# Branch and output projections of a diffusion block as three rounded products in place of plain fp32

## What is computed

```python
def branch_merge(y_a, y_b, y_c, gates, w_pa, w_pb, w_pc, w_out):
    g_a, g_b, g_c = jnp.split(gates, N_BRANCHES, axis=-1)
    m = (jax.nn.sigmoid(g_a) * (y_a @ w_pa) + jax.nn.sigmoid(g_b) * (y_b @ w_pb)
         + jax.nn.sigmoid(g_c) * (y_c @ w_pc))
    return m @ w_out
...
for layer in range(DEPTH):
    hx = modulate(rms_norm(x, norm1_g[layer]), sh1, sc1)
    mx, mc = token_mixers(hx @ w_in[layer], hc @ w_in[layer], ...)   # three branches, then branch_merge
    x = x + g1 * mx
    hx = modulate(rms_norm(x, norm2_g[layer]), sh2, sc2)
    # layer 0: dense SwiGLU of 2816; layer 1: top 2 of 8 expert SwiGLUs of 3584
    x = x + g2 * f
return rms_norm(x, final_g)
```

## Time and profile before

| | |
|---|---|
| Median of 3 runs | 2270.48 us (2268.6 to 2272.04) |
| Profiled execution, time | 2268.39 us |
| Profiled execution, span from first to last instruction | 2266.5 us |
| Mean granted clock of TensorE | 0.968 |
| PE busy | 2140.1 us, 94% |
| POOL busy | 1272.5 us, 56% |
| DVE busy | 1147.7 us, 51% |
| ACT busy | 1051.7 us, 46% |
| Read from memory | 500.24 MB |

### The profile page before, as it was taken

One profiled execution on the slowest core, in us unless ns is written; L12 is line 12 of the kernel. 1 busy time (PEld: TensorE's weight loads), 2 busy tenths in 40 slices (PEclk: granted clock), 3 DMA queues, 4 the chain that ended last, 5 costly groups with the idle time before them and its releaser, 6 DMA issues.

```text
span 2266.5 us, 27521 instructions
## 1 busy us (share of the span) xinstructions
PE 2140.1 (94%) x10750; PEld 1589.7 (70%) x10751; DVE 1147.7 (51%) x1353; ACT 1051.7 (46%) x1139; POOL 1272.5 (56%) x466
## 2 busy tenths in 40 slices
PE   5988899998999998887998999999999999999997
PEld 3874577647788787864997777776767777776775
DVE  2146311231010103345324887878778787878776
ACT  4223322014212123323324766766666666766665
POOL 2300233114545443400421989988988989988996
PEclk8999999998999999898997999999999999999999
DMA  7325521222222222225445999989999999989993
GB/s 296 111 94 223 207 93 75 75 74 103 102 80 106 77 91 93 92 104 205 162 162 204 371 337 353 358 334 352 346 341 345 347 340 351 357 333 352 346 346 142
DMA packets 69640, 503.16 MB, mean 222 GB/s; under 512 B 7744, under 2 KB 7872, under 8 KB 9088
## 3 DMA queue, kind: packets, MB, share of 16 engines
q1 hardware_dynamic: 68976, 497.92, 58.8%
q0 software_dynamic: 528, 3.41, 0.4%
HBM read 500.24 MB, written 1.05 MB: 221 GB/s over the span
## 4 chain that ended last, share of the span: by engine, by line
PE 49%; POOL 32%; issue 12%; DVE 3%; DMA 2%; ACT 1%; SPq 0%; POOLq 0%; DVEq 0%; ACTq 0%
POOL moe_lo L482 31%; PE bank L756 12%; PE bank L758 11%; PE bank L757 11%; PE bank L771 7%; PE bank L784 2%; PE turned L955 2%; PE pv_bank L974 1%; DMA start_slab<-in_w_mod 1%; PE bank L934 1%; DVE s_mx L1859 1%; DMA slab<-in_w_in 1%; POOL w_lo L446 1%; ACT H_NEW L1359 0%; PE bank L939 0%
## 5 line engine op out<-in xcount | busy, mean ns | idle before, releaser
L482 POOL TENSOR_TENSOR moe_lo<-moe_slab,moe_hi 128x512 fp32r<-128x512 f32 x336 | 916.0, 2750 | 163.1 <-ACT moe_hi L1543 161.8
L482 DVE TENSOR_TENSOR moe_lo<-moe_slab,moe_hi 128x1536 fp32r<-128x1536 f32 x336 | 688.3, 2053 | 175.0 <-ACT moe_hi L1543 172.6
L446 POOL TENSOR_TENSOR w_lo<-slab,w_hi 128x2048 fp32r<-128x2048 f32 (+3 forms) x72 | 293.1, 4072 | 741.8 <-ACT w_hi L1316 741.7
L1543 ACT ACTIVATE moe_hi<-moe_slab 128x2048 fp32r<-128x2048 f32 x336 | 629.5, 1906 | 0.1
L756 PE MATMUL bank<-moe_hi,HE_HI 128*96 128x512 f32 x896 | 360.3, 402 | 1.3 <-POOL moe_lo L482 1.2
L758 PE MATMUL bank<-moe_hi,HE_LO 128*96 128x512 f32 x896 | 353.1, 394 | 0.0
L757 PE MATMUL bank<-moe_lo,HE_HI 128*96 128x512 f32 x896 | 351.7, 392 | 0.0
L756 PE MATMUL bank<-H_HI,w_hi 128*128 128x512 f32 (+1 forms) x880 | 325.6, 370 | 17.9 <-POOL H_LO L660 12.7
L757 PE MATMUL bank<-H_LO,w_hi 128*128 128x512 f32 (+1 forms) x880 | 321.9, 366 | 0.0
L758 PE MATMUL bank<-H_HI,w_lo 128*128 128x512 f32 (+1 forms) x880 | 321.8, 366 | 0.0
L1316 ACT ACTIVATE w_hi<-slab 128x2048 fp32r<-128x2048 f32 (+1 forms) x72 | 135.6, 1883 | 166.6 <-PE bank L758 147.8
(11 more groups left out here) (199 smaller groups left out, 2481.9 us busy)
## 6 DMA issues: line engine op xcount, KB each, us to landing
moe_slab<-in_moe_up SPq DMA_DIRECT2D x224, 1024.0 KB, 4.8
moe_slab<-in_moe_w SPq DMA_DIRECT2D x112, 1024.0 KB, 4.8
slab<-in_w_mod SPq DMA_DIRECT2D x40, 1024.0 KB, 4.8
slab<-in_w_in SPq DMA_DIRECT2D x38, 1024.0 KB, 4.8
slab<-in_ffn_w SPq DMA_DIRECT2D x30, 1024.0 KB, 4.8
start_slab<-in_w_mod SPq DMA_DIRECT2D x8, 1024.0 KB, 18.0
slab<-in_w_proj SPq DMA_DIRECT2D x8, 1024.0 KB, 6.9
slab<-in_w_out SPq DMA_DIRECT2D x8, 1024.0 KB, 4.9
```

What stands on the lines that cost most here:

```text
L446: engine.tensor_tensor(lo, raw, hi.bitcast(F32), ALU.subtract).then_inc(done, 1)
L482: engine.tensor_tensor(moe_lo[n][:, blocks, :], moe_slab[k % MOE_RING][:, blocks, :], moe_hi[n][:, blocks, :].bitcast(F32), ALU.subtract). ...
L1543: af(moe_hi[k % MOE_SPLIT][:], moe_slab[k % MOE_RING][:], ACT.Copy).then_inc(moe_hi_ready, 1)
```

## The change

The branch and output slabs become split slabs: every slab except those for the modulation now passes through `w_hi` and `w_lo`, eight more in each layer, and in layer 1 DVE makes half of each low part. `Y` is cut into `Y_HI` (ACT, four instructions of two chunks) and `Y_LO` (DVE, four, in place of `Y`). `M` shrinks to two chunks that are used again for each j; ACT rounds them into `M_HI` and DVE subtracts into `M_LO`. PE makes three products where it made one. The first output slab is worked through for both halves up to chunk 5 before the last two chunks are waited for.

`M_LO` takes the place of `BIAS` and `POOL` in SBUF. So both are loaded for layer 1 again (the matrix thus twice in all), now from SP's queue after the last output slab of layer 0. Three slabs of the expert stream are loaded ahead of the last output slab's end, as the ring places come free, where it was four. The rounding of slab w3(0,0) moves behind the root in the norm; that of stream slab 1 too, in layer 1, with DVE's part of it between the norm's TMPs.

```diff
 def is_split(slab):
-    return slab[0] in ("in", "w1", "w3", "w2")
+    return slab[0] != "mod"
...
+SHARED += [(kind, 1, j) for kind in ("proj", "out") for j in range(4)]
...
+        Y_LO = at("Y_LO", 56, [P, DC, T], F32R)
+        Y_HI = at("Y_HI", 168, [P, DC, T], F32R)
-        M = at("M", 72, [P, DC, T])
+        M = at("M", 164, [P, 2, T])
+        M_HI = at("M_HI", 72, [P, DC, T], F32R)
+        M_LO = at("M_LO", 148, [P, DC, T], F32R)
...
             for n in range(1, len(order)):
+                if order[n] == ("w3", 0, 1):
+                    wait_full(sp, ("out", 0, 3, 1))
+                    sp.dma_start(POOL[:]..., a["pool_mat"]).then_inc(pool_in[1], 16)
+                    sp.dma_start(BIAS[:]..., a["rel_bias"][1]).then_inc(bias_in[1], 16)
                 load_slab(n, order[n])
...
-            wait_full(sp, ("gate", 1, 3, 2, 1))
-            for k in range(MOE_RING - RING):
+            for k in range(RING):
+                wait_parts(sp, ("out", 1, 4 - RING + k))
                 stream_load(k)
...
-                    (w,) = slab(("proj", layer, j))
+                    w = slab(("proj", layer, j))
                     if j == 0:
-                        pe.wait_ge(y_ready[layer], len(attention_pairs(layer)))
-                        ...
+                        pe.wait_ge(y_lo_ready[layer], DC // 2)
...
-                            filled(chain(out[:, 0:nq], [(w[:, k, P * m:P * m + P], Y[:, k, 0:nq]) ...
+                            filled(split_chain(out[:, 0:nq], [
+                                ([t[:, k, P * m:P * m + P] for t in w], [t[:, k, 0:nq] for t in (Y_HI, Y_LO)])
+                                for k in BRANCH_CHUNKS[b]]), key)
...
-                wait_taken(pe, ("proj", layer, 3, 2, 1))
+                w = slab(("out", layer, 0))
+                outs = [fill(("out", layer, 0, m)) for m in range(2)]
+                pe.wait_ge(m_lo_ready[layer], DC - 2)
+                for m in range(2):
+                    for k in range(DC - 2):
+                        out_products(outs[m], w, m, k)
+                for k in range(DC - 2, DC):
+                    pe.wait_ge(m_lo_ready[layer], k + 1)
+                    ...
...
-                if key == (1, 1):
+                if key in ((0, 2), (1, 1)):
                     high_part()
+                if key == (1, 2):
+                    stream_high(1)
...
+                for k in range(0, DC, 2):
+                    af(Y_HI[:, k:k + 2, 0:nq], Y[:, k:k + 2, 0:nq], ACT.Copy).then_inc(y_hi_ready[layer], 1)
...
-                        if 3 * j + b < 10:
-                            high_part()
+                        high_part()
+                    if j < 3:
+                        high_part()
+                        m_rounded(j)
+                    else:
+                        m_rounded(j)
+                        high_part()
...
-                squares((layer, 2), lo, hi, range(0, 4), out_added)
+                squares((layer, 2), lo, hi, range(0, 2), out_added)
+                high_part()
+                squares((layer, 2), lo, hi, range(2, 4), out_added)
+                high_part()
...
+                    if key == (1, 2) and c == 2:
+                        stream_low_part(dve, v, 1, slice(0, LO_DVE), moe_lo_dve)
...
+                    if norm_key == (1, 2) and c in (1, 3):
+                        low_half(("out", 1, 2 + c // 2))
...
+                for k in range(0, DC, 2):
+                    dve.wait_ge(y_hi_ready[layer], k // 2 + 1)
+                    v.tensor_tensor(Y_LO[:, k:k + 2, 0:nq], Y[:, k:k + 2, 0:nq], Y_HI[...], ALU.subtract)
...
+                    if j == 3:
+                        m_low()
+                    if layer == 1:
+                        low_half(slabs[4 * j + 5])
+                    if j < 3:
+                        m_low()
```

More of the change, by code:

```diff
@@ L704, in _ @@
             h_low_parts((1, 1))
-            for _ in range(2, 19):
+            for _ in range(2, 27):
                 next_low_part()
@@ L1481, in merge, with m_rounded @@
                 nq = S * len(streams_of(layer))
+                act.wait_ge(y_ready[layer], len(attention_pairs(layer)))
+                for p in range(2):
+                    wait_taken(act, ("poolw", layer, p))
+                for k in range(0, DC, 2):
+                    af(Y_HI[:, k:k + 2, 0:nq], Y[:, k:k + 2, 0:nq], ACT.Copy).then_inc(y_hi_ready[layer], 1)
+                def m_rounded(j):
+                    for m in range(2):
+                        wait_taken(act, ("proj", layer, j, 2, m))
+                        af(M_HI[:, 2 * j + m, 0:nq], M[:, m, 0:nq], ACT.Copy).then_inc(m_hi_ready[layer], 1)
                 for j in range(4):
@@ L1626, in out_added @@
                     wait_taken(act, ("out", layer, c // 2, c % 2))
-                squares((layer, 2), lo, hi, range(0, 4), out_added)
+                squares((layer, 2), lo, hi, range(0, 2), out_added)
+                high_part()
+                squares((layer, 2), lo, hi, range(2, 4), out_added)
+                high_part()
+                squares((layer, 2), lo, hi, range(4, 6), out_added)
                 if layer == 0:
@@ L1633, in _ @@
                     stream_high(0)
-                squares((layer, 2), lo, hi, range(4, 6), out_added)
-                if layer == 0:
-                    high_part()
-                else:
-                    stream_high(1)
                 squares((layer, 2), lo, hi, range(6, 8), out_added)
@@ L1906, in merge @@
                 nq = S * len(streams_of(layer))
-                gates = [W_IN_GATE + 4 * b + j for j in range(4) for b in range(3)]
+                slabs = []
+                for j in range(4):
+                    slabs += [("in", 1, W_IN_GATE + 4 * b + j) for b in range(3)] + [("proj", 1, j)]
+                slabs += [("out", 1, j) for j in range(2)]
                 if layer == 1:
-                    low_half(gates[0])
-                    low_half(gates[1])
+                    low_half(slabs[0])
+                    low_half(slabs[1])
+                for k in range(0, DC, 2):
+                    dve.wait_ge(y_hi_ready[layer], k // 2 + 1)
+                    v.tensor_tensor(Y_LO[:, k:k + 2, 0:nq], Y[:, k:k + 2, 0:nq], Y_HI[:, k:k + 2, 0:nq].bitcast(F32),
+                                    ALU.subtract).then_inc(y_lo_ready[layer], 1)
                 for j in range(4):
                     if layer == 1:
-                        for slab in gates[3 * j + 2:3 * j + 5]:
-                            low_half(slab)
+                        for key in slabs[4 * j + 2:4 * j + 5]:
+                            low_half(key)
                     for b in range(3):
```

76 lines of the change are left out of this document (45 added, 31 removed).

## The result

The changed kernel takes 2233.26 us, median of 4 runs (2228.61 to 2241.9), beside 2269.54 us for the kernel before (4 runs, 2268.34 to 2272.04): a ratio of 0.985 [0.981, 0.988]. The direction was right, the time was not. The same two kernels were run more often beside the experiments: in all 37 runs of before have a median of 2266.2 (2261.4 to 2272.0) and 9 of after one of 2235.3 (2228.2 to 2241.9). The difference of these is 30.9 us.

The account below looks back on a forecast made before the run. PE, busy 94% of the span, was taken as the bound. -34.9 + 1.5 + 0.6 + 0.2 + 2.6 + 0.4 = -29.6 us from 2268.39 gave 2238.8, and 2.1 for the median 2241; range 2235 to 2249.

Parts of the forecast that it names:

- PE's part, layer 0: Layer 0's four branch and four output slabs at the gate slabs' price: 23.1 us less, plus M's wait covered.
- (d): New products escape the 11 ns each gate matmul loses, 4 us in all: 2237; chance 0.03.
- (e): The new form brings PE nothing, as 48 loads of weights stand where 32 did: 2270; chance 0.03.
- Layer 1: Eight slabs 9.2 us less, M's wait 1.0 less; stalls for low parts add 0.6, 0.2 and 2.6.
- rival (c): Layer 1 becomes bound by conversions, each rounding 0.7 us later over 17 slabs: 12 us, 2253; chance 0.10.
- The norm after layer 0: Slab w3(0,0)'s low part stands ahead of H_LO in POOL's queue, so H_LO's first chunk and PE are later: +1.5 us.
- from there ... nothing gives the delay back: After H_LO's late first chunk PE is busy without a gap, at first at 1.2 GHz, so the 1.5 us stay.
- The norm before the experts: DVE's 1.75 us part of stream slab 1 between the TMPs delays H's chunk 2: about +0.4 us, bounds 0 and 1.75.
- rival (b): The expert stream misses its fourth slab loaded early: +3.1 us, 2244; chance 0.10.
- Rival (f): DVE and POOL exclude each other when both read two SBUF tiles, 4.6 us in each new layer 0 slab: +37, 2278; 0.04.
- M's subtractions end before the next low part starts: Layer 0's output phase: DVE's subtractions into M_LO finish before POOL's next low part, an argument against DVE and POOL excluding each other.
- The median of the runs stands 2.1 higher, so I predict 2241: Last step: the profiled execution less 29.6 us gives 2238.8; the runs' median stands 2.1 above it, hence 2241.

Follow-up runs that it names:

- DVE's larger share: The changed kernel with DVE making three quarters, not half, of each gate, branch and output slab's low part in layer 1: 2232.96 us, ratio 0.986 to the kernel before.
- The two orders on POOL: The changed kernel (2235.3 us), and the same with POOL making H_LO's first chunks ahead of slab w3(0,0)'s low part in layer 0's second norm: 2235.03 us.
- the two halves: Kernel before with only branch projections as three rounded products, 2252.64 us; with only output projections so, plus the second loads for layer 1, 2245.0 us.

## Why the prediction was right in its steps and wrong in its time

**PE's part, layer 0.** Forecast 24.7 (23.1 and 1.6 of M's wait), measured 24.7 in all three traces of the change; from the first branch product to the last output product 184.7 us, forecast 185. The plain slabs' prices in the chain and the gates' spacing were enough. Rivals (d) and (e) fall with the 226 ns.

**Layer 1.** Forecast -9.2 - 1.0 + 0.6 + 0.2 + 2.6 = -6.8, measured -5.8; first branch product to last output product 103.4, forecast 102. The waits for w_lo in the output phase are 1.9 and 0.6, forecast 2.0 and 0.6. The missing 1 us is no single term. By the starts of the products in the first pair, products and M's wait give 9.9 (forecast 10.2), the second and fourth output slab come 2.2 and 0.8 late (2.6 together in the forecast), and the shorter delays are 2.9 beside 2.0 before (forecast +0.8). PE's busy time fell by 7.6 and not by 9.2, since most of the short delays stand in the rows as longer matmuls (as 0.39 beside 0.28 in the earlier trace rows). With DVE's larger share the stage is 9.6 shorter than before, nearly the full 10.2. So rival (c) names the right resource; it had 12 us more than the sum, and 1 was measured.

**The norm after layer 0.** Forecast +1.5, and at equal clock (13.7 us at 1.2 GHz in both) the FFN's first product starts 12.7 us after the last output product did, 11.3 to 11.5 before: +1.3. (Counted from that product's end, as the forecast of 12.4 was, it is 12.3.) But the first SiLU is only 0.75 later. The step "from there ... nothing gives the delay back" failed by half. The stretch at 1.2 GHz lasts from 3.2 to 16.8 us after the last output product's start before the change and from 2.9 to 16.6 after it, so a first product at 11.5 finds 5.4 us of it and one at 12.7 finds 3.9; at 0.44 each that is an estimated 0.7 given back. In the two other traces of the change the slow stretch is 10.2 and the first SiLU no later than before (23.2). The two orders on POOL come out level because slab w3(0,0)'s own low part has a due time too.

**The norm before the experts.** Forecast +0.4, measured +0.9 at equal clock (34.25 against 33.4), inside its bounds of 0 and 1.75. The loads: neither FFN nor stream became longer, so rival (b) and the second loads of `BIAS` and `POOL` cost nothing that shows.

**Rival (f), exclusion of DVE and POOL.** It is there, off PE's path. Timelines of DVE and POOL in the changed kernel's layer 0, two subtractions of M and the low part of a slab beside them:

```profile
397.07 5.29 DVE L1990 TENSOR_TENSOR M_LO<-M,M_HI 128x512 fp32r<-128x512 f32 x2 [1.04 <-ACT M_HI L1520]
...
396.60 4.61 POOL L456 TENSOR_TENSOR w_lo<-slab,w_hi 128x2048 fp32r<-128x2048 f32 x1 [5.86 <-ACT w_hi L1343]
```

The row merges two subtractions: the first takes 4.69 and ends 0.55 after POOL does, the second 0.68. The prediction's "M's subtractions end before the next low part starts" is thus wrong for three of the eight, the first of each pair but the last; nobody waits for these, as the output slabs come 40 us later and more. The last pair, which is wanted soonest, ran alone (0.69 each).

**The sum.** Stage by stage: -24.7 - 5.8 + 0.75 + 0.9 = -28.9, beside -29.6 forecast, -30.9 between the medians of 37 and 9 runs, and -36.3 between the medians of the first four runs of each. The forecast of the edit was right; what made the first pair 36 was in no term of it.

**The step that failed** is the last one: "The median of the runs stands 2.1 higher, so I predict 2241", with the range made from the terms of the edit alone. Two things are wrong in it. It took three runs (2268.6 to 2272.0) for the kernel's level, which over 37 runs is 2266.2; -29.6 from there is 2236.6. And it gave no width to stages that the change does not touch. Those differ between executions of one kernel by 6.1 us (start) and 2.9 (FFN), with the microseconds at 1.2 GHz; the sum put these stages at nothing, and the first pair of traces has 8.5 us in them. Single runs of the changed kernel lie from 2228.2 to 2241.9, four of nine below 2230, and a median of four moves with them: that of all nine, 2235.3, would have lain in the range, at its very edge. The profile of before had the sign of it: a clock of 0.64 to 0.92 in four stages, 148 us at 1.2 GHz in all. With 2236.6, the 5 us to either side by which runs of before scatter and the 3 us of the edit's own bounds, the range would have been 2229 to 2245. The traces show that the clock makes the difference in the FFN within a kernel, and idle work in the waits takes it out there; for the start it accounts for a part. Why one execution gets more of it than another after the same wait is open, and so is whether an edit shifts it: the medians of the two halves lie 2.3 and 3.5 us off the sums of their stages, to opposite sides. Open is also why the first four runs of before are all above 2268, as only 8 of the 33 later ones are: chance or the chip they ran on.

## What to carry to other kernels

Price a replaced instruction by the spacing of one with the same shapes and types in the same trace; here that gave 24.7 us of 24.7. Before giving a time, look at the clock column of the stages that the change does not touch: here the clock fell behind some of the waits of 2.8 us between stretches of matmuls and not behind others, and one kernel's time differed from itself by 10 us, so the level wants many runs and the range that width. Compare the edited stages between two traces, not the totals; and when a conversion is split between DVE and POOL, price it as the sum of both parts, since here they took turns, and give the larger share to the faster one (DVE's 1536 elements took 1.76 us, POOL's 512 1.26).

## What the runs showed of the hardware

- A wait of 2.8 us on PE was followed by 0, 3.4 or 6.8 us at 1.2 GHz in traces of unedited kernels, with PE equally busy around it (11.15 of 14 us).
- 51 idle products (two recorded instructions each) in the waits of norms and FFN made the kernels 7 us (the change) and 13 us (before) faster.
- DVE and POOL took turns when both subtracted two SBUF tiles, and the one that began first went first. With DVE 0.04 us ahead POOL's 512 elements took 2.86 us beside DVE's 1.76, and 1.26 in the norm's H_LO. With POOL 0.47 us ahead DVE's subtraction, 0.69 alone, took 4.69 and ended 0.55 after POOL's 4.61.
